# Moving a probability copy ahead of a decay, a tanh ahead of a split, and a small load, in a one-core two-block transformer kernel

## What is computed

```python
f = swiglu(rms_norm(h, ffn1_pre_g), ffn1_w_gu, ffn1_w_down)
h = h + 0.5 * rms_norm(f, ffn1_post_g)
# mixer, the parts that the change touches
xc = causal_depthwise_conv(x_br, conv_w, conv_b)
r, i = sigmoid(blocks(xc, w_a) + b_a), sigmoid(blocks(xc, w_x) + b_x)
a = exp(-8 * r * softplus(-lam))              # "decay"
bterm = sqrt(1 - a * a) * (i * xc)            # i * xc is "gate input"
y_lru = scan(a, bterm) * gelu(gate_br)
probs = softmax(window_scores with sinks)     # turned (transposed), then times v
merged = sigmoid(g_lru) * (y_lru @ w_proj_lru) + sigmoid(g_attn) * (y_attn @ w_proj_attn)
h = h + rms_norm(merged @ w_out, mix_post_g)
f = swiglu(rms_norm(h, ffn2_pre_g), ffn2_w_gu, ffn2_w_down)
```

## Time and profile before

| | us |
|---|---|
| three runs | 1303.57, 1304.58, 1304.84 |
| median | 1304.58 |
| the profiled execution, its own time | 1303.98 |
| its span in the profile | 1302.2 |
| PE busy | 1296.9 |
| PE weight loads busy | 1102.5 |
| DVE busy | 895.2 |
| ACT busy | 707.5 |

### The profile page before, as it was taken

The page is one execution under the profiler, slowest core; times in us unless marked ns, Lnnn a source line. Parts: engine busy times, 40 slices in busy tenths (PEclk is TensorE's granted clock), DMA queues, the critical chain, the costliest instruction groups (busy, mean ns, idle before and its releaser), DMA issues.

```text
span 1302.2 us, 18174 instructions
## 1 busy us (share of the span) xinstructions
PE 1296.9 (100%) x7332; PEld 1102.5 (85%) x7332; DVE 895.2 (69%) x1032; ACT 707.5 (54%) x976; POOL 87.2 (7%) x77
## 2 busy tenths in 40 slices
PE   9999999999999999999999999999999999999999
PEld 7888888987788888888888999888888889998887
DVE  6576556697978755547767567855776766587575
ACT  6464445568746544435766544544467665444451
POOL 0000000000001000000252000000002610000000
PEclk9999999999999999999999999999999999999999
DMA  9685637542376866644655543466666564345562
GB/s 341 212 300 173 203 109 243 159 130 82 129 260 209 276 186 187 190 148 149 204 181 184 172 143 118 146 195 181 191 193 224 166 209 146 111 136 159 178 193 82
DMA packets 64963, 234.42 MB, mean 180 GB/s; under 512 B 7664, under 2 KB 7792, under 8 KB 64752
## 3 DMA queue, kind: packets, MB, share of 16 engines
q1 hardware_dynamic: 62064, 224.42, 53.7%
q10 hardware_dynamic: 2816, 8.84, 1.9%
HBM read 232.19 MB, written 1.05 MB: 179 GB/s over the span
## 4 chain that ended last, share of the span: by engine, by line
PE 94%; DVE 3%; ACT 1%; issue 0%; DMA 0%; POOL 0%; another core or an unknown queue 0%; ACTq 0%; DVEq 0%; POOLq 0%
PE psum L1952 24%; PE psum L1973 23%; PE psum L1953 23%; PE psum L1958 5%; PE psum L2020 5%; PE psum L2005 5%; PE psum L1959 5%; PE psum L2153 2%; PE psum L2407 1%; DVE w_lo L1205 1%; PE psum L2253 1%; PE psum L2393 0%; PE psum L2170 0%; DMA raw<-weights 0%; DVE scores_max L1383 0%
## 5 line engine op out<-in xcount | busy, mean ns | idle before, releaser
L1205 DVE TENSOR_TENSOR w_lo<-raw,w_hi 128x1024 fp32r<-128x1024 f32 x219 | 265.7, 1222 | 127.5 <-ACT w_hi L624 126.0
L624 ACT ACTIVATE w_hi<-raw 128x1024 fp32r<-128x1024 f32 x219 | 230.1, 1055 | 139.7 <-PE psum L1973 105.0
L1952 PE MATMUL psum<-w_hi,x_hi 128*128 128x512 f32 x552 | 217.8, 395 | 0.0
L1953 PE MATMUL psum<-w_hi,x_lo 128*128 128x512 f32 x552 | 214.7, 389 | 0.0
L1205 DVE TENSOR_TENSOR y_lo<-raw,y_hi 128x1024 fp32r<-128x1024 f32 x139 | 168.9, 1221 | 60.7 <-ACT y_hi L624 60.0
L624 ACT ACTIVATE y_hi<-raw 128x1024 fp32r<-128x1024 f32 x139 | 146.4, 1056 | 76.4 <-PE psum L1973 50.5
L1973 PE MATMUL psum<-w_lo,x_hi 128*128 128x512 f32 x552 | 170.1, 389 | 0.0
L1952 PE MATMUL psum<-y_hi,x_hi 128*128 128x512 f32 (+1 forms) x376 | 148.1, 394 | 0.0
L1953 PE MATMUL psum<-y_hi,x_lo 128*128 128x512 f32 (+1 forms) x376 | 146.3, 389 | 0.0
L1952 PEld LDWEIGHTS psum<-w_hi,x_hi 128*128 128x128 f32 x552 | 103.8, 188 | 22.5 <-issue 1.6
L1973 PEld LDWEIGHTS psum<-w_lo,x_hi 128*128 128x128 f32 x552 | 103.6, 188 | 22.0 <-DVE w_lo L1205 0.7
(11 more groups left out here) (219 smaller groups left out, 2286.7 us busy)
## 6 DMA issues: line engine op xcount, KB each, us to landing
raw<-weights SPq DMA_DIRECT2D x406, 512.0 KB, 4.1
probs<-weights SPq DMA_DIRECT2D x8, 512.0 KB, 5.3
probs_t<-weights SPq DMA_DIRECT2D x8, 512.0 KB, 5.0
arena<-gains ACTq DMA_DIRECT2D x7, 512.0 KB, 5.0
arena<-gate_bias ACTq DMA_DIRECT2D x2, 1536.0 KB, 7.4
norm<-x_feat SPq DMA_DIRECT2D x4, 256.0 KB, 5.1
res<-x SPq DMA_DIRECT2D x2, 512.0 KB, 9.0
arena<-lru_w ACTq DMA_DIRECT2D x1, 1024.0 KB, 5.5
```

The lines of the kernel that those rows point to most:

```text
L624: act.activation(slot(t)[0], raw_place(t), ACT.Copy).then_inc(hi_ready, 1)
L1205: dve.tensor_tensor(lo, raw_place(t), hi.bitcast(F32), ALU.subtract).then_inc(lo_ready, 1)
L1952: pe.matmul(out_, l_hi, r_hi, start=start, stop=False, skip_group_check=skip)
L1953: pe.matmul(out_, l_lo, r_hi, start=False, stop=False, skip_group_check=skip)
```

## The change

It has four parts.

1. The load of the identity goes from ACT's queue, second in it, to SP's queue behind the load of tile 3, in front of the two loads of `res`.
2. In the second feed-forward, `swish(1, 0, 1)` on ACT and `swiglu(1, 0, (1,))` on DVE stand in front of `refill(base + 2)` instead of behind it.
3. In the mixer, `decay(0)` on ACT and `gate_input(0)` on DVE go from the end of chunk 7 to chunk 8, behind the `probs_copy` at its head. `decay(1)` and `gate_input(1)` stay where they are.
4. `warm` runs five products of zeros instead of six.

```diff
@@ sync
                 if t == 3:
+                    sp.dma_start(cst[:, C_IDENT:C_GAIN], consts[:, C_IDENT:C_GAIN]).then_inc(ident_loaded, 16)
                     for tok in range(TOK):
@@ scalar, ffn(1, ...)
                     refill(base + 1)
+                    swish(1, 0, 1, base)
                     refill(base + 2)
-                    swish(1, 0, 1, base)
                     refill(base + 4)
@@ scalar, start
-            act.dma_start(cst[:, C_IDENT:C_GAIN], consts[:, C_IDENT:C_GAIN]).then_inc(ident_loaded, 16)
@@ scalar, mixer
                     probs_copy(At(u))
+                if c == 8:
+                    decay(0)
                 if c == 7:
@@ scalar, mixer, behind refill(t + 3)
                     decay_tanh(c - 7)
-                    decay(c - 7)
+                if c == 8:
+                    decay(1)
@@ vector, ffn(1, ...)
                     refill(base + 1)
+                    swiglu(1, 0, (1,))
                     refill(base + 2)
-                    swiglu(1, 0, (1,))
@@ vector, mixer
                     probs_copy(At(u), 8)
+                if c == 8:
+                    gate_input(0)
@@ vector, mixer, behind refill(t + 3)
-                if c in (7, 8):
-                    gate_input(c - 7)
+                if c == 8:
+                    gate_input(1)
@@ tensor
-            warm(6)
+            warm(5)
```

## The result

The changed kernel takes **1308.67 us** (median of seven runs, 1308.11 to 1310.22) against 1304.54 us before (seven runs beside it). The ratio is 1.0033, 95% interval 1.0024 to 1.0042: slower by 4.1 us. The profiled execution took 1308.67 us with a span of 1306.9, so the spans differ by 4.7 us.

What follows compares the result with a forecast made beforehand. PE, with 94% of the chain that ended last, was taken to bound the kernel. Start -0.2, mixer +2.0 and feed-forward +1.7 gave +3.5 us, from the median 1304.58 a forecast of 1308.1 us, range 1305.9 to 1309.9.

Steps and rivals of the forecast that it cites:

- Both large terms: The delays forecast for PE in the mixer, +2.0 us, and in the second feed-forward, +1.7 us.
- Mixer, +2.0 taken: Mixer: the decay behind the copy delays line 931, which PE waits for before F_I1; +2.0 us.
- some 2.3: Mixer: PE's expected wait in us at F_I1's loads for line 933 (931 before).
- The bounds, 1.9 to 2.1: Mixer: range of the delay in us, from the next product starting at 300.0 to 300.2 instead of 298.13.
- a wait that is already there means no room at all: All three places: where PE already waits, whatever delays the releaser delays PE by as much.
- DVE's half at 0: Mixer: moving gate_input(0) on DVE costs nothing, falling into DVE's 5.00 us wait for line 851.
- Feed-forward, +1.7 taken: Second feed-forward: later splits delay the load of base + 17; +1.7 us, the middle of 0.8 and 2.6.
- the 4.1 and 5.9 of the bounds: Second feed-forward: load times in us for base + 17, the median of all loads and the load issued at that moment before.
- the first wait lies inside the second: Second feed-forward: the 0.7 us at the down product is contained in the later load's delay, so not added.
- Start, -0.2 taken: Start: the later identity lets tile 1 land sooner, one zero fewer is worth 0; -0.2 to 0 us, -0.2 taken.
- PE's wait near 10.48, which should have come at 10.3: Start: PE's wait at 10.48, hanging on tile 1's landing, was to come some 0.2 us sooner.
- Rival C: Start: without the sixth product of zeros the clock rises later, slowing tile 0; +1.7 us, total 1309.8; chance 0.13.

Runs made afterwards that it cites:

- the tanh of F_GL0 sooner: Kernel before, with ACT's tanh of F_GL0 ahead of the copy of the turned probabilities in chunk 8: 1304.32 against 1304.39 us, ratio 1.0004.
- the low part sooner: Full change, with DVE's hidden_rest (low part of the hidden values) one split earlier in the second feed-forward: 1308.59 against 1304.39 us, ratio 1.0035.
- the start alone: Kernel before with parts 1 and 4 only (identity behind tile 3, five zeros): 1304.33 against 1304.39 us, ratio 1.0001.
- DVE's half of part 3: Kernel before with only gate_input(0) moved behind DVE's copy of the turned probabilities: 1304.28 against 1304.25 us, ratio 1.0002.
- the feed-forward alone: Kernel before with part 2 only, on ACT and DVE: 1306.30 us, ratio 1.0014.
- the version with the decay in the gap: Full change, with decay(0) moved on behind ACT's split in chunk 8, into ACT's idle time: 1306.09 against 1304.52 us, ratio 1.0016.
- the mixer alone: Kernel before with part 3 only, on ACT and DVE: 1306.28 against 1304.56 us, ratio 1.0012.
- the decay behind line 931: Kernel before with part 3 only, but decay(0) behind ACT's tanh of F_GL0 and ahead of the tanh of F_R1: 1305.92 us, ratio 1.0012.
- identity alone: Kernel before with part 1 only, the identity loaded by SP behind tile 3: 1304.38 against 1304.25 us, ratio 1.0002.
- the decay in the gap (part 3 alone): Kernel before with part 3 only, but decay(0) behind ACT's split in chunk 8: 1304.09 against 1304.56 us, ratio 0.9998.

## Why the prediction was right, and where it was not

It said 1308.1 us, and 1308.67 was measured. Both large terms came from the waits that it named, in the places that it named.

- **Mixer, +2.0 taken, 1.92 measured.** The price of the decay was 2.09 us from the earlier trace rows, its first start to the start of the copy. There the copy had to wait for the transposes. Where the next instruction waits for nothing, it starts 1.97 us behind the decay's start (295.45 to 297.42), 0.09 ahead of its last end. The landmarks came as written: a wait of 2.22 for "some 2.3", ACT idle 2.12, the copies released together. The bounds, 1.9 to 2.1, held.
- **The step that was wrong in kind:** "a wait that is already there means no room at all". For line 931 it was not so. The run with the tanh of F_GL0 sooner removed its 0.27 us and won nothing; the wait for line 869, 0.20 us, was the one that counted. The forecast survived because the decay stands in front of both.
- **DVE's half at 0:** shown in the run with that half alone; as predicted, DVE's wait for the transposes grew (1.26 to 2.39 us) and its later one shrank (5.00 to 3.86).
- **Feed-forward, +1.7 taken, 1.84 measured.** The load went out 1.15 us later by the tanh (437.00 - 433.15 = 3.85, against 433.76 - 431.06 = 2.70), and took 5.1 us instead of 4.4, between the 4.1 and 5.9 of the bounds. The two make up the 1.84. That the first wait lies inside the second is shown by the run with the low part sooner. The 1.84 is counted from a profile in which PE waited 0.45; in other profiles without part 2 the load landed sooner or later and the stretch was 9.95 to 10.96 us, in those with it 12.09 to 12.28. So part 2 costs 1.1 to 2.3 us, depending on when that load would have landed. The middle, 1.7, is what was forecast. That the load would go out later was worked out; how long it would take was a guess half way between two rows, so that the figure is so close is partly luck.
- **Start, -0.2 taken, +0.17 in this profile, and nothing in the runs.** The term was finer than what it was read from: with five or six zeros the mixer's entry scatters from 293.18 to 294.00 us, whether the start is changed or not. So 0.2 us either way is neither shown nor excluded. Tile 0 did land 0.2 sooner, but PE's wait near 10.48, which should have come at 10.3, came at 10.62, the second feature and tile 1 having landed later (rows below). With the start alone it did come at 10.31, and the time was still that of before.

```profile
6.59 0.91 ACT L666 ACTIVATE x_hi<-norm,cst 128x256 fp32r<-128x256 f32 x2 [0.65 <-DMA norm<-x_feat]
8.25 1.06 ACT L625 ACTIVATE w_hi<-raw 128x1024 fp32r<-128x1024 f32 x1 [0.75 <-DMA raw<-weights]
```

- **Rival C** was rightly a rival and rightly not the forecast: its slow first tile comes with three zeros fewer, and not with one.
- **What the prediction lacked:** the wait in the first layer. In the changed kernel two weight loads of the first layer landed late, and ACT, DVE and PE followed:

```profile
975.57 1.06 ACT L625 ACTIVATE w_hi<-raw 128x1024 fp32r<-128x1024 f32 x1 [0.97 <-DMA raw<-weights]
977.20 1.06 ACT L625 ACTIVATE y_hi<-raw 128x1024 fp32r<-128x1024 f32 x1 [0.56 <-DMA raw<-weights]
```

The same two waits for DMA were 0.37 and 0.32 in the profile of before. The wait is 1.03 with the start alone and 1.16 with DVE's half of part 3, both of which cost nothing that the time can tell, and 0.54 in the feed-forward alone. The profile of before has the lowest of all fourteen. These runs do not show it to be an effect of the change.

**What stays open.** The parts alone add up to 1.72 + 1.74 - 0.06 = 3.4 us, the change has 4.1, and the version with the decay in the gap lies 2.6 below the change, not 1.9. Each of these differences is known to about 1.2 us only, by the intervals, so the missing 0.7 us may be nothing. A share of it may be real: in both kernels with the mixer's delay and the old feed-forward (the mixer alone, the decay behind line 931) the load of base + 17 landed in time, so that PE did not wait its 0.45 us there. If so, the mixer's delay alone is paid for in part by that wait, and with part 2, where the load is late in any case, nothing is paid back. This is not shown: one of the seven other profiles without part 2 shows the same without any delay in the mixer (the start alone), so it may be chance.

## What to carry to other kernels

An instruction that fills an engine's wait is free only there. Behind the thing waited for, it stands ahead of everything that follows, so look for the next wait on that engine that is as long as the instruction: the decay cost 1.9 and 1.6 us in two places and nothing in the third. Of two short waits in a row only one may count; ask of each what its releaser itself had waited for. And a split made one place later also postpones the next load into its buffer, which is where the time goes when the loads have no lead.

## What the runs showed of the hardware

- Loads of 512 KB issued 1.14 us apart took 3.7 and 5.1 us in the changed kernel. With the same code around it, the split of base + 17 started 0.6 us sooner (start alone) and 0.6 later (identity alone) than in the profile of before, counted from the tanh. A single row of a landing is good to about that much here.
- The pace of the first tile changed from one profile to the next with the same six zeros: 0.23 us a product from the first on in the earlier trace rows, slow for two products with the decay in the gap (part 3 alone), whose start is that of before, and slow for three with the identity alone (below). The zeros themselves took from 4.3 to 5.5 us in the nine profiles that have six.

```profile
6.29 0.33 PEld L1952 LDWEIGHTS psum<-w_hi,x_hi 128*128 128x128 f32 x1
...
7.15 0.29 PEld L1952 LDWEIGHTS psum<-w_hi,x_hi 128*128 128x128 f32 x1
7.48 0.19 PEld L1953 LDWEIGHTS psum<-w_hi,x_lo 128*128 128x128 f32 x1
```

- The granted clock in the table of windows did not show this. With three zeros it reads 1.00 for the stretch from 6 to 9 us, in which every product took 0.43 us. At the very start of this kernel the pace has to be read from the loads. The row of the table:

```profile
6.00:9.00 3.00, 2.82 (x7) 2.27 (x8) 2.21 (x4) 2.12 (x5) 0.00 (x0) 1.00 1.01 388
```

The columns are the stretch and its length, the busy time (and count) of PE, PEld, DVE, ACT and POOL, the granted clock, the DMA share and GB/s.
